# One half of the picks first, its expert rows summed during the other half's, and a third of the rows summed on the matrix engine

## The chip, the cores and the metric

The kernel runs on one core of a Trainium2 chip (trn2). The metric is the device time of one execution in microseconds (us). Five engines work beside each other: TensorE (PE; its weight loads are PEld in the profile), VectorE (DVE), ScalarE (ACT), GpSimd (POOL) and SyncE (SP). They meet only at semaphores. Transfers between device memory and the on-chip arena are made by 16 DMA engines; SP's queue issues those with fixed addresses, POOL's those that gather rows by an index.

## The reference, cut to what matters

A layer over T = 256 tokens of width D = 2048: a mixing half (RWKV scan, short convolution, projections), which the change does not touch, and then an expert half, in which each token picks 8 heads x 16 experts = 128 of 16384 experts:

```python
q = (h @ w_q)...; s1 = q[...,0,:] @ sub_keys_1; s2 = q[...,1,:] @ sub_keys_2
v1, i1 = top_k(s1, 16);  v2, i2 = top_k(s2, 16)          # per token and head
top, pos = top_k(v1[:, None] + v2[None, :], 16)           # of 256 sums
eidx = i1 * 128 + i2 (at pos);  gate = softmax(top)
act = gelu(einsum('td,tkd->tk', h, expert_u[eidx]))       # 128 dots per token
ff  = einsum('tk,tkd->td', gate * act, expert_v[eidx])    # 128 rows of 2048 summed per token
out = x + gate2 * rms_norm(ff, post_ffn_w)
```

Everything is float32. The 256 tokens are two blocks b of 128 tokens, one token on each partition. For each block and each k of 128, one gather brings one row per partition: 128 rows of `expert_v` are 1 MB, 256 gathers 256 MB.

## The kernel before

After the mixing half (about 800 us) the expert half runs in stages, and each engine's program is a fixed list with waits, so its order is the order of the source.

- Queries and routing. PE makes queries and scores in four groups g; ACT writes the scores (L752). DVE runs `route(b, g)` eight times (L1460 to L1507: MAX8, FIND_INDEX8, MATCH_REPLACE8 and small ops), each yielding 32 of the 256 indices (b, k).
- Dots. Of each `expert_u` row, 1152 columns are gathered by POOL (L544) into a ring of `UROWS` = 6 slots and multiplied with h by DVE (`dots`, L1527; 256 of them, numbered n). Between two routes stand 16 dots. The first `EARLY` = 48 take h from the arena (`junk`), the others from PSUM. The other 896 columns are done densely: SP loads 128 tiles (`product_tile`, 448 KB each, 4 slots), PE multiplies each with h of all 256 tokens (L1161) and ACT evacuates the result to `dense` (L761), 32768 columns of the arena.
- Picks. From `dense` the products of a token's own experts must be picked. In steps q of four tokens PE spreads the first keys (`spread_keys`, L1175, bfloat16), ACT turns them into one-hot rows (L775, L777), PE multiplies these with `dense` (L1189, float32, 4 matmuls) and DVE picks by the second key (`pick`, L1535). Two PSUM banks alternate in each of these. There are 64 steps; in every second one stands one of the last 32 dots (`LATE` = 224 - 128 = 96 of block 1).
- Sums. DVE adds both parts (L1558), ACT applies Gelu (L781), and DVE multiplies with the gates (L1563). Then for b in 0, 1 and k in 0..127: a gathered row of `expert_v`, times its weight, is added to sums in PSUM (L1573). POOL gathers into 12 slots of `v_row`, 8 of which lie in `dense`; its first gather waits for all 64 pick steps (`y_ps`), and each later one for the sum that frees its slot.
- End of a block: ACT takes squares and the root (L788 to L792), DVE scales and adds x (L1580, L1582), SP stores. x is parked in `out` and read back once `dense` is done with.

Of the kernel before, what the change touches and what calls it, by code (L numbers as in the profile page):

```python
# [99 lines left out]
def build_layer(nc, x, cols, ada, w_in, w_tail, lora_up, keys,  # L100
                u_dense, u_rows, expert_v, out):
    with ExitStack() as ctx:
# [100 lines left out]
        gw1 = new(D)  # L203
        junk = new(D)
# [3 lines left out]
        scores = [view(arena_size - (2 - b) * D, KC, NKEYS) for b in range(TB)]  # L208
# [6 lines left out]
        dense = view(dense_at, NKEYS, T)  # L215
        top[0] = ring_at
        tile_at = [take(KU * P), take(KU * P)]
        val1T = new(T)
        assert take(0) >= ring_at + SL
# [22 lines left out]
        gate, idx1f, idx2f = (view(front_at + n * TB * KTOP, TB, KTOP) for n in range(3))  # L242
        q_slot = [ring[:, 7, :], view(yT_at, D), view(yT_at + D, D), gw1]
        v_at = [g_at + (2 + n) * D for n in range(8)] + [row_at + n * D for n in range(4)]
        assert v_at[-1] + D <= dense_at and v_at[7] + D <= arena_size
        v_row = [view(a, D) for a in v_at]
        gw2, ff = view(dense_at, D), view(dense_at + D, D)
        assert dense_at + 2 * D <= g_at
# [60 lines left out]
        v_sum = sem("v_row_summed")  # L309
# [23 lines left out]
        def _(sp):  # L333
# [84 lines left out]
            sp.dma_start(xs[:, :, :], rows_of(out)).then_inc(x_in, 16)  # L418
            for tb in range(TB):
                for h in range(2):  # L420
                    c = slice(h * D // 2, (h + 1) * D // 2)
                    sp.wait_ge(fin_v, 4 * tb + 2 * (h + 1))
                    sp.dma_start(out[tb * P:(tb + 1) * P, c], xs[:, tb, c]).then_inc(stored, 16)
# [3 lines left out]
        def _(pool):  # L427
# [145 lines left out]
        def _(act):  # L573
# [168 lines left out]
            for g in range(4):  # L742
# [11 lines left out]
            for j in range(NKEYS):  # L754
                act.wait_ge(tile_ps, j + 1)
                if dense_at + (j + 1) * T > g_at and dense_at + j * T <= g_at:
                    act.wait_ge(stored, 16)
                    act.wait_ge(u_dot, EARLY)
                if dense_at + j * T == arena_size - 2 * D:
                    act.wait_ge(picked, 8)  # L760
                nc.scalar.activation(dense[:, j, :], bank(5 + j % 2, 0, T), ACT.Copy).then_inc(tile_out, 1)  # L761
# [8 lines left out]
            for q in range(T // 4):  # L770
# [8 lines left out]
            for b in range(TB):  # L779
                act.wait_ge(act_done, b + 1)  # L780
                nc.scalar.activation(wv[:, b, :], actv[:, b, :], ACT.Gelu).then_inc(gelu_done, 1)  # L781
            act.wait_ge(gw2_ps, 1)
            nc.scalar.activation(gw2, ps[:, 0:2048], ACT.Copy).then_inc(gw2_out, 1)
            for b in range(TB):
                act.wait_ge(v_sum, (b + 1) * KTOP)
                if b:
                    act.wait_ge(fin_v, 4 * b)
                nc.scalar.activation(ff, ps[:, 2048 - b * 2048:4096 - b * 2048], ACT.Square, accum_out=ss[:, 12 + b:13 + b]).then_inc(fin_a, 1)  # L788
# [3 lines left out]
                nc.scalar.activation(rstd[:, 12 + b:13 + b], lns[:, 12 + b:13 + b], ACT.Exp, scale=-0.5).then_inc(fin_a, 1)  # L792

        @block.tensor
        def _(pe):
# [297 lines left out]
            def rows(col, b0):  # L1093

                for k in range(KC):
                    last = mm(bank(b0 + k // 4, k % 4 * P, k % 4 * P + P), col[:, k:k + 1].broadcast_to([P, P]), ident, start=True, stop=True)
# [7 lines left out]
            p2.done(rows(gcol[:, 0, :], 2), "gate1")  # L1104
# [73 lines left out]
            pe.wait_ge(u_dot, KTOP)  # L1178
            spread_keys(0)
            for q in range(T // 4):  # L1180
                if q + 1 < T // 4:
                    spread_keys(q + 1)
# [5 lines left out]
                for i in range(4):  # L1188
                    last = mm(bank(5 + q % 2, i * P, (i + 1) * P), hot[q % 2][:, i, :], dense[:, :, 4 * q + i], start=True, stop=True)  # L1189
                last.then_inc(y_ps, 1)  # L1190

            pe.wait_ge(picked_out, T)
            pe.wait_ge(idxT_out, 1)
            for b in range(TB):
                last = nc.tensor.transpose(bank(7, b * P, (b + 1) * P), val1T[:, b * P:(b + 1) * P], ident)
            last.then_inc(valT_ps, 1)
            pe.wait_ge(u_dot, TB * KTOP)
            rows(gcol[:, 1, :], 0).then_inc(gw2_ps, 1)

        @block.vector  # L1200
        def _(dve):
# [256 lines left out]
            def top16(src, vals, where, rep):  # L1458
# [4 lines left out]
                r(V.match_replace(rep, vals[:, 0:8], src, NEG))  # L1463
                settle()
                r(V.max(vals[:, 8:16], rep))
                settle()
                r(V.max_index(where[:, 8:16], vals[:, 8:16], rep))  # L1467

            def route(b, g):

                dve.wait_ge(sc_out, 2 * g + b + 1)
                for c in range(4):
                    top16(scores[b][:, 4 * g + c, :], v16[:, c, :], u32(iu[:, c, :]), repl[:, c * NKEYS:(c + 1) * NKEYS])
# [7 lines left out]
                for h in range(2):  # L1481
                    top16(cand[:, h, :], topv[:, h, :], u32(pos[:, h, :]), repl[:, h * 256:(h + 1) * 256])
# [12 lines left out]
                for half, sel, dst in ((0, hi_f, idx1f), (1, lo_f, idx2f)):  # L1495
# [3 lines left out]
                    for h in range(2):  # L1499
                        e = eq[:, h * TOPK:(h + 1) * TOPK, :]  # L1500
                        r(tt(e, e, deep(i16[:, 2 * h + half, :]), ALU.mult))
                    settle()
# [17 lines left out]
            def dots(b, lo, hi):  # L1520

                for k in range(lo, hi):
                    n = b * KTOP + k
# [138 lines left out]
```

## Time and profile before

| | us |
|---|---|
| median of 3 runs (2208.21 to 2212.54) | 2210.57 |
| the profiled execution: its own time | 2209.84 |
| its span from first to last instruction | 2208.1 |
| DVE busy over the span | 1599.6 (72%) |
| PE busy | 1393.6 (63%) |
| POOL busy | 658.9 (30%) |
| ACT busy | 352.0 (16%) |
| DMA, mean over the span | 308 GB/s |

The profile's instants are us from the start of the span. Shares over the whole span mix stages with different limits, so the stages are read one by one: which engine is full, what rate the DMA moves, and what ended each wait. A float32 matmul is recorded as two instructions on PE. A DVE operation with an accumulator shows a short second record (DVE_READ_ACCUMULATOR); the distance of two starts is what one costs.

### The profile page before, as it was taken

Reading aid. Unit: us, or ns where it says so; the run is one execution under the profiler, and the core shown is the slowest. Engines: PE = TensorE matmul, PEld = TensorE weight load, DVE = VectorE, ACT = ScalarE, POOL = GpSimd, SP = SyncE. Lnnn points to the kernel's source line nnn. Section 1 sums busy time; section 2 is a strip of 40 time slices with the busy share of each in tenths; the row PEclk is TensorE's granted clock in tenths of the full one; section 3 lists DMA queues with packets and bytes.
Section 4 is the critical chain, followed back from the end, with each engine's and each line's share of the span. In section 5 each row is a group of like instructions: output and inputs, shape, how many; then the busy total and the mean of one; then the engine's idle time right before and its main releaser. Section 6 shows DMA issues by size and latency. Waiting matters only on the chain.

```text
span 2208.1 us, 20312 instructions
## 1 busy us (share of the span) xinstructions
PE 1393.6 (63%) x7103; PEld 1189.2 (54%) x7103; DVE 1599.6 (72%) x2429; ACT 352.0 (16%) x702; POOL 658.9 (30%) x707
## 2 busy tenths in 40 slices
PE   4799999999998989999999990499000000000000
PEld 4688888888885468888888880498000000000000
DVE  5945555655654023777778669988999998999998
ACT  2032222222221011011111120266000000000000
POOL 1022332213320001433322446422433333333331
PEclk8899999999999999999999995699555555555555
DMA  9936654565546553799998999854999999999995
GB/s 398 383 145 234 248 215 171 189 265 221 188 183 253 189 191 137 283 353 358 356 357 342 373 409 412 315 151 135 423 422 422 422 422 421 422 422 421 422 422 240
DMA packets 122001, 680.99 MB, mean 308 GB/s; under 512 B 13488, under 2 KB 13616, under 8 KB 65840
## 3 DMA queue, kind: packets, MB, share of 16 engines
q0 software_dynamic: 73728, 419.46, 47.1%
q1 hardware_dynamic: 47760, 257.97, 30.5%
q10 hardware_dynamic: 416, 2.25, 0.3%
q8 instruction: 62, 1.02, 0.2%
q14 instruction: 35, 0.29, 0.0%
HBM read 675.44 MB, written 4.19 MB: 308 GB/s over the span
## 4 chain that ended last, share of the span: by engine, by line
PE 38%; DMA 30%; DVE 27%; issue 2%; ACT 1%; POOL 1%; DVEq 0%; ACTq 0%; POOLq 0%
DVE ps L1573 15%; DMA arena<-in_u_rows,arena 15%; PE ps L868 14%; DMA arena<-in_expert_v,arena 13%; PE ps L1189 5%; PE ps L917 5%; PE ps L946 4%; DVE arena L1527 3%; DVE arena L1238 2%; PE ps L1087 2%; PE ps L951 2%; DMA arena<-in_ada 1%; PE ps L960 1%; DVE arena L1467 1%; DVE arena L1462 1%
## 5 line engine op out<-in xcount | busy, mean ns | idle before, releaser
L1573 DVE SCALAR_TENSOR_TENSOR ps<-arena,ps 128x2048 f32<-128x2048 f32 x256 | 602.8, 2355 | 36.3 <-DMA arena<-in_expert_v,arena 6.1
L1161 PE MATMUL ps<-arena 128*128 128x256 f32 x1792 | 387.1, 379 | 0.0
L544 POOL DMA_INDIRECT arena<-in_u_rows,arena x256 | 248.6, 971 | 444.7 <-DVE arena L1527 390.3
L1161 PEld LDWEIGHTS ps<-arena 128*128 128x128 f32 x1792 | 340.3, 190 | 46.5 <-DMA arena<-in_u_dense 0.3
L544 POOL DMA_INDIRECT arena<-in_expert_v,arena x256 | 239.9, 937 | 410.5 <-DVE ps L1573 380.0
L868 PE MATMUL ps<-arena 128*128 128x256 f32 x1440 | 339.3, 379 | 0.0
L1527 DVE SCALAR_TENSOR_TENSOR arena<-arena,ps 128x1152 f32<-128x1152 f32 x208 | 279.4, 1355 | 78.8 <-DMA arena<-in_u_rows,arena 74.4
L868 PEld LDWEIGHTS ps<-arena 128*128 128x128 f32 x1440 | 262.0, 190 | 29.4
L1189 PE MATMUL ps<-arena 128*128 128x128 f32 x512 | 124.9, 399 | 88.7 <-DVE ps L1535 86.3
L1189 PEld LDWEIGHTS ps<-arena 128*128 128x128 f32 x512 | 98.9, 207 | 93.3 <-DVE ps L1535 86.5
L1217 DVE SCALAR_TENSOR_TENSOR arena<-arena 128x2048 f32<-128x2048 f32 x60 | 142.8, 2381 | 0.0
L655 ACT ACTIVATE arena<-ps 128x512 f32<-128x512 f32 x144 | 81.7, 585 | 294.2 <-PE ps L951 116.3
L917 PE MATMUL ps<-arena 128*128 128x512 f32 x256 | 112.6, 593 | 1.5 <-DVE arena L1398 1.5
L1087 PE MATMUL ps<-arena 128*128 128x256 f32 x512 | 111.3, 379 | 0.0
L1358 DVE TENSOR_TENSOR arena<-ps,arena 128x512 f32<-128x512 f32 x40 | 27.7, 692 | 110.5 <-PE ps L946 110.5
L788 ACT ACTIVATE arena<-ps 128x2048 f32<-128x2048 f32 x2 | 3.8, 1877 | 642.9 <-DVE ps L1573 642.9
L1087 PEld LDWEIGHTS ps<-arena 128*128 128x128 f32 x512 | 96.9, 190 | 13.0
L761 ACT ACTIVATE arena<-ps 128x256 f32<-128x256 f32 x128 | 49.2, 384 | 339.5 <-PE ps L1161 339.5
L946 PE MATMUL ps<-arena 128*128 128x128 f32 x704 | 96.3, 280 | 4.3 <-ACT arena L655 3.1
L946 PEld LDWEIGHTS ps<-arena 128*128 128x128 f32 x704 | 89.0, 191 | 17.9 <-ACT arena L655 8.0
L1527 DVE SCALAR_TENSOR_TENSOR arena<-arena 128x1152 f32<-128x1152 f32 x48 | 64.4, 1360 | 45.1 <-DMA arena<-in_u_rows,arena 44.8
L517 POOL TENSOR_TENSOR arena<-arena 128x512 f32<-128x512 f32 x40 | 61.9, 1547 | 92.7 <-PE ps L946 92.7
(248 smaller groups left out, 1577.4 us busy)
## 6 DMA issues: line engine op xcount, KB each, us to landing
arena<-in_ada SPq DMA_DIRECT2D x96, 1024.0 KB, 5.0
arena<-in_u_dense SPq DMA_DIRECT2D x128, 448.0 KB, 6.9
arena<-in_w_in SPq DMA_DIRECT2D x45, 1024.0 KB, 6.7
arena<-in_w_tail SPq DMA_DIRECT2D x32, 1024.0 KB, 6.9
arena<-in_w_in SPq DMA_DIRECT2D x12, 512.0 KB, 16.7
arena<-in_u_rows,arena POOLq DMA_INDIRECT x256, 9.1
arena<-in_expert_v,arena POOLq DMA_INDIRECT x256, 25.4
arena<-in_x ACTq DMA_DIRECT2D x1, 2048.0 KB, 15.0
```

What stands on the lines that cost most here:

```text
L517: gm.done(tt(LTm[m % 2][:, :, :], LT[:, :, :], lmask[:, m:m + 1, :].broadcast_to([P, NCH, P]), ALU.mult), f"m{m}")
L544: nc.gpsimd.indirect_dma_start(out=row, out_offset=None, in_=table[:, :], in_offset=bass.IndirectOffsetOnAxis(ap=i32(idx[:, b, k:k + 1]), ...
L655: am.done(A(out, in_, func, **kw), name)
L868: last = mm(bank(b, 0, T), w[:, k, :], hT[:, k, :], start=(k == 0), stop=(k == KC - 1))
L917: last = mm(bank(OUT_BANKS[g][b]), yT[:, OUT_K[n], b * P:(b + 1) * P], w, start=(n == 0), stop=(n == KC - 1))
L946: last = mm(bank(b, c * P, c * P + P), l[:, c, :], r[:, c, :], start=True, stop=True)
L1087: last = mm(bank(b0 + s // 2, (s % 2) * T, (s % 2) * T + T), w[:, kk, s * P:(s + 1) * P], h2T[:, k, :], start=(k == 0 and s % 2 == 0), sto ...
L1161: last = mm(bank(5 + j % 2, 0, T), u_tile[j % len(u_tile)][:, k, :], h2T[:, k, :], start=(k == 0), stop=(k == KU - 1))
L1189: last = mm(bank(5 + q % 2, i * P, (i + 1) * P), hot[q % 2][:, i, :], dense[:, :, 4 * q + i], start=True, stop=True)
L1217: ins = stt(dst, ring[:, slot, :], silu_c[:, k:k + 1], dst, ALU.mult, ALU.add)
L1527: stt(row, row, 1.0, h, ALU.mult, ALU.mult, accum_out=actv[:, b, k:k + 1]).then_inc(u_dot, 1)
L1573: stt(sums_ps, v_row[n % len(v_row)], wv[:, b, k:k + 1], sums_ps, ALU.mult, ALU.add).then_inc(v_sum, 1)
```

## The change

Three things in the expert half. (1) `dense` is laid out as two halves, one per block, so the 32 pick steps of block 0 come first and free the first half; they carry 44 of the last 48 dots (`LATE` is now 256 - 48 = 208). Then block 0's activations and weights are made, and each pick step of block 1 is followed by three rows of block 0's sum. (2) Every third row (k % 3 == 2; 42 rows of block 0, 33 of block 1) is summed by PE: ACT scales the identity by the weights (`diagonal`), PE multiplies the row with it in four matmuls of 512 columns, accumulating in four PSUM banks, and DVE adds these banks to its own sum (`merge`), which now lies in the arena (`total`). (3) Dots stand inside `route`, two at 11 of 14 places, instead of 16 between routes. There are 13 row slots; three wait only for the last tile's product, four for the last dot, six for block 0's picks. Slots, scores, x and gate rows lie elsewhere, with waits to match.

```diff
+        dense = view(dense_at, TB, NKEYS, P)
+        diag = [view(front_at + 3 * TB * KTOP + T + n * P, P) for n in range(2)]
+        total = [view(half_at[0] + b * D, D) for b in range(TB)]
+        v_at = [0, D, ring_at] + [row_at + n * D for n in range(4)] + [half_at[0] + (TB + n) * D for n in range(6)]
+        V_EARLY, V_TILE = 7, 3
# POOL
                 if n == 0:
-                    pool.wait_ge(y_ps, T // 4)
-                if n == 8:
+                    pool.wait_ge(tile_ps, NKEYS)
+                if n == V_TILE:
                     pool.wait_ge(u_dot, TB * KTOP)
+                if n == V_EARLY:
+                    pool.wait_ge(y_ps, P // 4)
                 if n >= len(v_row):
-                    pool.wait_ge(v_sum, n - len(v_row) + 1)
+                    before = n - len(v_row)
+                    if on_pe(before):
+                        pool.wait_ge(d_sum, pe_rows(before) + 1)
+                    else:
+                        pool.wait_ge(v_sum, before - pe_rows(before) + 1)
# ACT
+                if g == 0:
+                    act.wait_ge(stored, 16)
...
-                if dense_at + (j + 1) * T > g_at and dense_at + j * T <= g_at:
-                    act.wait_ge(stored, 16)
+                if j == (junk_at - half_at[1]) // P:
                     act.wait_ge(u_dot, EARLY)
...
+            def diagonal(b, m):
+                d = b * PE_ROWS[0] + m
+                if d >= 2:
+                    act.wait_ge(d_sum, d - 1)
+                k = 3 * m + 2
+                nc.scalar.activation(diag[d % 2], ident, ACT.Copy, scale=wv[:, b, k:k + 1]).then_inc(diag_out, 1)
...
+            for q in range(P // 4 + 1):
+                one_hot(q)
+            gelu(0)
+            act.wait_ge(wv_done, 1)
+            for m in range(PE_ROWS[0]):
+                if P // 4 + 1 + m < T // 4:
+                    one_hot(P // 4 + 1 + m)
+                if m == P // 4 + 4:
+                    gelu(1)
+                diagonal(0, m)
+            act.wait_ge(wv_done, 2)
+            for m in range(PE_ROWS[1]):
+                if m == 4:
+                    norm(0, merged, 2)
+                    act.wait_ge(gw2_ps, 1)
...
+                diagonal(1, m)
+            norm(1, v_sum, TB * KTOP - sum(PE_ROWS))
# PE
+            def diagonal_row(b, m):
+                n = b * KTOP + 3 * m + 2
+                pe.wait_ge(diag_out, b * PE_ROWS[0] + m + 1)
+                pe.wait_ge(v_land[n % len(v_row)], 16 * (n // len(v_row) + 1))
+                for c in range(4):
+                    last = mm(bank(SUM_BANKS[b][c]), diag[(b * PE_ROWS[0] + m) % 2], v_row[n % len(v_row)][:, c * GROUP:(c + 1) * GROUP],
+                              start=(m == 0), stop=(m == PE_ROWS[b] - 1))
+                last.then_inc(d_sum, 1)
...
+            turn_products(0, 7)
+            for q in range(P // 4, T // 4):
+                if q + 1 < T // 4:
+                    spread_keys(q + 1)
+                key_rows(q)
+                if q == P // 4:
+                    pe.wait_ge(u_dot, TB * KTOP)
+                    pe.wait_ge(act_done, 1)
+                diagonal_row(0, q - P // 4)
# DVE
+            def some_dots():
+                calls[0] += 1
+                if calls[0] % 14 % 4 != 3:
+                    dots(ndot[0], ndot[0] + 2)
+                    ndot[0] += 2
             for c in range(1, 8):
-                dots(0, (c - 1) * 16, c * 16)
-                route(c // 4, c % 4)
+                route(c // 4, c % 4, some_dots)
+            dots(ndot[0], LATE)
...
+            for q in range(P // 4):
+                pick(q)
+                if q in (2, 4):
+                    gate_sums(q // 2 - 1)
+                more = 2 if q % 8 in (1, 4, 6) else 1
+                dots(ndot[0], ndot[0] + more)
+                ndot[0] += more
+            activations(0, 7)
+            dots(ndot[0], TB * KTOP)
+            weights(0)
+            for m in range(P // 4):
+                pick(P // 4 + m)
+                for k in range(3 * m, 3 * m + 3):
+                    add_row(0, k)
...
+            merge(0)
+            for k in range(KTOP):
+                if k == 12:
+                    finish(0)
+                if k == 3 * PE_ROWS[1] + 9:
+                    merge(1)
+                add_row(1, k)
+            finish(1)
+PE_ROWS = (KTOP // 3, 33)
+SUM_BANKS = ((2, 3, 4, 7), (0, 1, 5, 6))
```

`add_row` is the former sum (a plain multiply for k = 0) and passes over the rows that PE takes. The two MEMSETs of the PSUM sums are gone.

## Rows read from the trace of the kernel before

**Rows 1.** The page, second part: DMA rate in 40 slices of 55.2 us.
```profile
GB/s 398 383 145 234 248 215 171 189 265 221 188 183 253 189 191 137 283 353 358 356 357 342 373 409 412 315 151 135 423 422 422 422 422 421 422 422 421 422 422 240
```
**Rows 2.** Windows: from:to, length, busy of PE, PEld, DVE, ACT, POOL; clock, DMA, GB/s.
```profile
1200.00:1220.00 20.00, 20.00 (x95) 17.60 (x94) 19.04 (x71) 2.31 (x6) 1.90 (x3) 1.00 0.80 300
1240.00:1260.00 20.00, 20.00 (x95) 17.60 (x94) 11.25 (x19) 2.41 (x7) 8.45 (x9) 1.00 1.03 410
1440.00:1460.00 20.00, 20.00 (x121) 18.21 (x121) 17.73 (x91) 14.11 (x20) 4.70 (x5) 1.00 0.49 149
1900.00:2100.00 200.00, 0.00 (x0) 0.00 (x0) 191.19 (x82) 0.00 (x0) 76.39 (x82) 0.50 1.01 422
2180.00:2190.00 10.00, 0.00 (x0) 0.00 (x0) 9.58 (x5) 0.00 (x0) 0.00 (x0) 0.50 0.19 80
```
**Rows 3.** The page, fifth part: costliest groups.
```profile
L1573 DVE SCALAR_TENSOR_TENSOR ps<-arena,ps 128x2048 f32<-128x2048 f32 x256 | 602.8, 2355 | 36.3 <-DMA arena<-in_expert_v,arena 6.1
L1217 DVE SCALAR_TENSOR_TENSOR arena<-arena 128x2048 f32<-128x2048 f32 x60 | 142.8, 2381 | 0.0
L917 PE MATMUL ps<-arena 128*128 128x512 f32 x256 | 112.6, 593 | 1.5 <-DVE arena L1398 1.5
L1358 DVE TENSOR_TENSOR arena<-ps,arena 128x512 f32<-128x512 f32 x40 | 27.7, 692 | 110.5 <-PE ps L946 110.5
```
**Rows 4.** Timeline of all engines at both ends of the sums: start, length, what.
```profile
1536.38 0.94 POOL L544 DMA_INDIRECT arena<-in_expert_v,arena  x1 [20.54 <-PE ps L1189]
...
2194.95 1.88 ACT L788 ACTIVATE arena<-ps 128x2048 f32<-128x2048 f32 x1 [322.85 <-DVE ps L1573]
```
**Rows 5.** Timeline: ACT's first scores; then DVE's dots, one route, picks.
```profile
844.69 0.60 ACT L752 ACTIVATE arena<-ps 128x512 f32<-128x512 f32 x1 [6.67 <-PE ps L1135]
...
933.05 1.36 DVE L1527 SCALAR_TENSOR_TENSOR arena<-arena 128x1152 f32<-128x1152 f32 x1
...
1199.45 0.29 DVE L1460 MAX8 arena<-arena 128x8 f32<-128x128 f32 x1
...
1216.89 1.35 DVE L1527 SCALAR_TENSOR_TENSOR arena<-arena,ps 128x1152 f32<-128x1152 f32 x1
...
1218.16 1.35 DVE L1527 SCALAR_TENSOR_TENSOR arena<-arena,ps 128x1152 f32<-128x1152 f32 x1
...
1409.98 0.35 DVE L1535 SCALAR_TENSOR_TENSOR ps<-arena,ps 128x128 f32<-128x128 f32 x1
...
1410.25 0.35 DVE L1535 SCALAR_TENSOR_TENSOR ps<-arena,ps 128x128 f32<-128x128 f32 x1
```
**Rows 6.** Source views: tiles, x's store, row gathers (ns min/median/max, first and last start).
```profile
L1161 PE MATMUL ps<-arena x1792: 379/379/483, 930.1 to 1316.9; 128*128 128x256 f32 x200
...
L406 SPq DMA_DIRECT2D out<-arena x1: 399/399/399, 800.5 to 800.5; - x1
...
DMA to landing us min/median/max: 14.2/14.2/14.2
...
L544 POOL DMA_INDIRECT arena<-in_expert_v,arena x256: 932/939/948, 1536.4 to 2165.3; - x128
```
**Rows 7.** Timelines of DVE and of POOL: dots from the arena, gathers beside them.
```profile
985.14 1.36 DVE L1527 SCALAR_TENSOR_TENSOR arena<-arena 128x1152 f32<-128x1152 f32 x1 [0.38 <-DMA arena<-in_u_rows,arena]
...
986.69 1.36 DVE L1527 SCALAR_TENSOR_TENSOR arena<-arena 128x1152 f32<-128x1152 f32 x1 [0.19 <-DMA arena<-in_u_rows,arena]
...
985.87 1.44 POOL L544 DMA_INDIRECT arena<-in_u_rows,arena  x1 [0.30 <-issue]
987.61 1.25 POOL L544 DMA_INDIRECT arena<-in_u_rows,arena  x1 [0.30 <-issue]
```
**Rows 8.** Windows, columns as in Rows 2: PE in a pause, at half clock, at full.
```profile
800.00:802.00 2.00, 0.00 (x0) 0.00 (x0) 1.83 (x4) 1.94 (x5) 0.00 (x0) 0.50 0.98 410
...
804.00:806.00 2.00, 2.00 (x11) 2.00 (x10) 0.67 (x1) 0.00 (x0) 0.00 (x0) 0.50 1.10 369
...
808.00:810.00 2.00, 2.00 (x12) 1.79 (x11) 2.00 (x5) 2.00 (x5) 0.00 (x0) 1.00 0.98 410
```

More of the change, by code:

```diff
@@ L203, in build_layer @@
         gw1 = new(D)
+        junk_at = take(0)
         junk = new(D)
@@ L207, in build_layer @@
         qT = view(q_at, KC, T)
-        scores = [view(arena_size - (2 - b) * D, KC, NKEYS) for b in range(TB)]
+        scores = [view(arena_size - (1 - b) * NKEYS * P - D, KC, NKEYS) for b in range(TB)]
         i32 = lambda v: v.bitcast(I32)
@@ L1091, in groups, with rows @@
                         score(g - 1)
-            def rows(col, b0):
+            def rows(col, banks):
                 for k in range(KC):
-                    last = mm(bank(b0 + k // 4, k % 4 * P, k % 4 * P + P), col[:, k:k + 1].broadcast_to([P, P]), ident, start=True, stop=True)
+                    last = mm(bank(banks[k // 4], k % 4 * P, k % 4 * P + P), col[:, k:k + 1].broadcast_to([P, P]), ident, start=True, stop=True)
                 return last
@@ L1103, in _ @@
             pe.wait_ge(v2.sem, v2.at("ga1"))
-            p2.done(rows(gcol[:, 0, :], 2), "gate1")
+            p2.done(rows(gcol[:, 0, :], (2, 3, 4, 5)), "gate1")
             for g in range(1, 4):
@@ L1188, in _ @@
                 for i in range(4):
-                    last = mm(bank(5 + q % 2, i * P, (i + 1) * P), hot[q % 2][:, i, :], dense[:, :, 4 * q + i], start=True, stop=True)
+                    b, t = divmod(4 * q + i, P)
+                    last = mm(bank(5 + q % 2, i * P, (i + 1) * P), hot[q % 2][:, i, :], dense[:, b, :, t], start=True, stop=True)
                 last.then_inc(y_ps, 1)
-            pe.wait_ge(picked_out, T)
-            pe.wait_ge(idxT_out, 1)
-            for b in range(TB):
-                last = nc.tensor.transpose(bank(7, b * P, (b + 1) * P), val1T[:, b * P:(b + 1) * P], ident)
@@ L1200, in _ @@
+            turn_products(1, 0)
+            for m in range(P // 4, PE_ROWS[0]):
+                diagonal_row(0, m)
+            pe.wait_ge(act_done, 2)
+            for m in range(PE_ROWS[1]):
+                diagonal_row(1, m)
+                if m == 1:
+                    pe.wait_ge(merged, 2)
+                    rows(gcol[:, 1, :], SUM_BANKS[0]).then_inc(gw2_ps, 1)
         @block.vector
@@ L1456, in _, with top16 @@
             NEG = -3.0e38
-            def top16(src, vals, where, rep):
+            def top16(src, vals, where, rep, between):
                 r(V.max(vals[:, 0:8], src))
@@ L1501, in route @@
                         r(tt(e, e, deep(i16[:, 2 * h + half, :]), ALU.mult))
+                    between()
                     settle()
@@ L1518, in gate_sums, with dots @@
                 settle()
-            def dots(b, lo, hi):
-                for k in range(lo, hi):
-                    n = b * KTOP + k
+            def dots(lo, hi):
+                for n in range(lo, hi):
+                    b, k = divmod(n, KTOP)
+                    if n == EARLY:
+                        dve.wait_ge(h_ps, 1)
                     row = u_row[n % UROWS]
@@ new lines, in merge, with finish @@
+            def merge(b):
+                dve.wait_ge(d_sum, sum(PE_ROWS[:b + 1]))
+                dve.wait_ge(v_sum, nsum[0])
+                at = 0
+                for lo, hi in ((2, 5), (7, 8)) if b == 0 else ((0, 2), (5, 7)):
+                    c = slice(at, at + (hi - lo) * GROUP)
+                    tt(total[b][:, c], ps[:, lo * GROUP:hi * GROUP], total[b][:, c], ALU.add).then_inc(merged, 1)
+                    at = c.stop
+                dve.wait_ge(merged, 2 * (b + 1))
+            def finish(b):
@@ L1598, with on_pe, pe_rows @@
 EARLY = 48
-LATE = KTOP - T // 8
+LATE = TB * KTOP - 48
+PE_ROWS = (KTOP // 3, 33)
+SUM_BANKS = ((2, 3, 4, 7), (0, 1, 5, 6))
+def on_pe(n):
+    b, k = divmod(n, KTOP)
+    return k % 3 == 2 and k < 3 * PE_ROWS[b]
+def pe_rows(n):
+    return sum(on_pe(i) for i in range(n))
 def kernel(x, c, ada_w, ada_b, pre_mix_w, post_mix_w, w_in, rwkv_mix, w0, w_up, a0, a_up, g_up, k_k, k_a, r_k,
```

123 lines of the change are left out of this document (63 added, 60 removed).

## Prediction

> **What bounds the kernel now.** I began with the DMA rate in slices [rows 1]: from slice 29 on, a third of the span, it stands at 422 GB/s, and it falls to 151 and 135 in the two slices just before. So I asked stage by stage which engine was full and whether the DMA was [rows 2]. Four stages matter:
> - Routing and dots, to about 1217. PE is busy all the time (the tiles), while DMA moves 300 GB/s beside a route and 410 beside dots: the ring of 6 fills while DVE routes, and then nothing asks.
> - Dots alone, 1217 to 1410: DMA at 412 in the slice from 1325 [rows 1], DVE waits for rows. DMA-bound.
> - Picks, 1410 to 1537: PE full, DVE 89%, DMA at 149 GB/s. PE-bound; DMA half idle.
> - Sums: DMA at 422 and DVE at 96% [rows 2]. One row is 1.049 MB, so DMA needs 2.485 us a row, and DVE 2.355 [rows 3] plus about 0.10 between two, 2.46. Both are bounds within 1%, so quicker sums alone can gain only DVE's lag: the last row has landed at about 2182 (0.19 of the window that begins at 2180 [rows 2]), DVE ends at 2195 [rows 4].
>
> What a gain must come from is therefore DMA time that is idle before the sums, from 1410 to 1537 and beside the routes.
>
> **Part 1, routing between dots.** A route is 17.4 us (1199.45 to 1216.89), a dot 1.28 (start to start) [rows 5]. Now a route carries 22 dots: 17.4 + 22 x 1.28 = 45.6 us of DVE, 2.07 us a dot. DMA beside the tiles: a tile takes (1316.9 - 930.1) / 128 = 3.02 us [rows 6] for 0.459 MB, 152 GB/s; of 410 [rows 2] 258 are left, and a row of 0.590 MB takes 2.29 us. So DMA, not DVE, sets the pace, if the ring never runs dry. At 933 the kernel before starts dot 21 [rows 5]; with dots in the route by then done (DVE allows up to 28) I take 25. Then (1317 - 933) / 2.29 = 168 more by the last tile, 193; the 15 left to dot 208 at 0.590 MB / 412 GB/s = 1.43 us end at 1338. Before, dot 224 ended at 1409.98 [rows 5], dot 208 thus at 1410 - 16 x 1.43 = 1387. Bounds: 1336 and 1387 (no gain, if dots in program order wait for rows while routing queues behind them). I take 1348, near the first, since DVE has 10% slack but the ring covers only 6 rows. Two waits are added or moved here. ACT's wait for x's store stands before the scores, and routing and PE's next scores wait behind it; the store lands at 815 and the scores come at 844.7 [rows 5, 6]: 30 us of cover, nothing. The wait for dot 48 stands before tile 29, at 933 + 29 x 3.02 = 1020, dot 48 comes at 933 + 23 x 2.29 = 986: 34 us of cover; past it, PE's tiles would stop and all behind them.
>
> **Part 2, block 0's picks.** A pick is 0.27 [rows 5]. DVE: 128 x 0.27 + 44 x 1.28 + the two gate sums (three small operations each, estimated at 1.1 from the route's small ones) = 34.6 + 56.3 + 2.2 = 93 us. PE takes 1.98 us a step (91 DVE records in 20 us at 18 for two steps [rows 2]), 63 us: covered. So DVE sets it, and DMA again has slack (44 rows in 93 us). Row gathers begin once the gather of dot 256 is out, which waits for dot 250: 1348 + 90 = 1438, where they began at 1536.4 [rows 4]. Three rows fit before the last dots end; those come after block 0's activations, some 7 us behind the picks, and row 4 may be late by 3 us.
>
> **Part 3, the sums.** Before, first gather to last landing took 2182 - 1536.4 = 645.6 us, 636 of rows and the rest x read back and a store. These stay. With DMA the bound, the last row lands at 1438 + 645.6 + 3 = 2087. Each three rows give 7.455 us; what must fit in:
> - DVE, with block 1's picks: 4 x 0.27 + 2 x 2.48 (arena form, 2.381 [rows 3], plus 0.10) = 6.0. It fits.
> - PE: a 512-column matmul is two instructions of 112.6 / 256 = 0.44 [rows 3], 8 of them 3.5 us, and a pick step 1.98: 5.5. It fits at full clock.
> - ACT: two passes over the one-hot rows and a diagonal, under 2 us. Free.
> - POOL: a gather is 0.94 [rows 6] and 0.30 of issue [rows 7]: 3 x 1.24 = 3.7. It fits.
> - Slots: 13 x 2.485 = 32 us round; a row is held up to 7 us by DVE or PE, which leaves ten in flight. `finish(0)`, the gate rows (PE) and `norm(0)` (ACT, with later diagonals queued behind it, and PE's rows behind those) hold some for perhaps 15 us; before, the same steps stood between two sums, and no slice there leaves 422 [rows 1].
>
> At the end PE has left; DVE takes 29 rows alone at 2.48 against 2.485, with `merge(1)` in the way: 4 x 0.69 [rows 3] = 2.8. So the last sum ends 2.4 + 2.8 = 5.2 after the last landing, where it was 13. From there to the end 2208.1 - 2194.95 = 13.2 [rows 4], unchanged.
>
> **Sum.** 2087 + 5.2 + 13.2 = 2105.4 of span, 103 under 2208.1: about 39 from the routes, 59 from the picks (net of dots moved into them), 8 from DVE's lag, less 3. The profiled execution's own time is 1.7 above its span, and it is 0.7 under the median: 2107 us.
>
> **Gathers beside sums from the arena.** In the kernel before, a gather that is issued while DVE runs a dot with both inputs in the arena is stretched: 1.44 and 1.25 us, each ending 0.81 after the dot did [rows 7]. Beside the present sums, with one input in PSUM, the longest of 256 took 0.948 [rows 6]. The new sums have both in the arena, so a gather waits for up to one sum. It gets through at the dot's end, with 0.19 us before the next one [rows 7]; so one passes per sum, and 2 per three rows plus two in the 2.5 us that DVE has left. That is 4 for 3 needed, and I cost it at nothing.
>
> The Trainium skill, "SBUF — State Buffer", section "Who interferes with whom", says that a DVE instruction with two SBUF inputs and a GpSimd instruction that reads SBUF shut each other out for a whole instruction. The stretched gathers agree, with their 0.81 us after the dot; that DVE is shut out in turn, no row here shows. By the rule alone the gathers would be late, which is rival B.
>
> **Rivals.**
> A. TensorE at half clock in block 1's picks. For: after a pause the clock was 0.50, and stayed so in a window in which PE was busy throughout, before it rose [rows 8]; in the new stage PE has gaps of 2 us each 7.5. Against: PE has some 75% to do there. At 1.2 GHz the row costs 7.0 and the step at least 1.98 (0.2 by the weight loads): 9.0 to 9.4 against 7.455, 32 times: 50 to 62 us, 2163. Behind the picks 7.0 still fits. The skill ("TensorE: Matmul & The Clock Gate", section "What's actually happening") has PE start at half clock after an idle spell and reach full after sustained work; by it each wait for a row could count, which is this case.
> B. The slower side: gathers get through only while DVE rests. Place: the gap of 0.10 us between two sums, half of the one seen. Price: three gathers need 3 x 1.24 of rest, so three rows take 4.96 + 3.72 = 8.7, 1.2 more than 7.455, 75 times, plus 16 rows at the end at 1.2: 110 us. 2217, slower by 0.3%. It decides when three rows cost more than about 8.6. Partial forms (gathers late, some bubbles) give 2120 to 2170.
> C. Dots in the routes bring nothing, because DVE waits in program order: 1387 for 1348, 2146.
> D. PE cannot hide its weight loads (8 x (0.85 + 0.2) at half clock, 8.4; with picks 10.6): 32 x 3.1 + 43 x 0.95 = 140 us, 2247.
>
> **How the numbers follow.** Forecast (DMA sets the pace, 2088 to 2130): 0.56; C and mixtures to 2150: 0.14; A: 0.12; B partial: 0.08; B full: 0.05; D: 0.05. Likeliest 2107. Low end 2088: dot 208 at 1336, no gap, merge hidden. High end 2170, past A; beyond are B in full and D. A measurement can tell 0.2%, some 4 us, from no change: faster 0.88, same 0.03, slower 0.09.
>
> **What would show it.** Right: DMA at 410 beside the routes without the dips to 300; the first pick near 1348; the first row gather near 1438; 422 GB/s from there to about 2087; POOL waiting for DVE and PE; clock 1.00 in block 1's picks. Wrong: DMA under 400 after the first rows. Then the waits tell: DVE for PE with clock 0.50 is A or D; gathers of 2 to 3 us with DVE waiting for landings is B; a first pick near 1387 is C.

## The result and the profile after

The changed kernel takes 2102.46 us (median of 4 runs, 2101.11 to 2104.54), the kernel before in the same comparison 2209.73 (2208.21 to 2212.54): a ratio of 0.951, 95% interval 0.950 to 0.953, or 107 us less. The forecast was 2107. The profiled execution, the slowest of the four, took 2104.54 us, its span 2102.7. The kernel before was timed again with each group of runs below (medians 2209.88, 2210.53 and 2211.90); each ratio is to the one of its own group, and differences of about 2 us between groups are not read.

The page of the changed kernel: DMA rate and granted clock in 40 slices of 52.6 us, and three groups of instructions (busy us, mean ns | idle before).

```profile
PEclk8899999999999999999999999677999988888865
...
GB/s 395 407 143 270 223 148 203 262 216 168 211 265 195 227 153 160 203 322 410 409 409 407 409 407 409 344 296 368 421 422 421 421 422 421 423 422 421 422 422 277
...
L1657 DVE SCALAR_TENSOR_TENSOR arena<-arena 128x2048 f32<-128x2048 f32 x179 | 420.8, 2351 | 125.8 <-DMA arena<-in_expert_v,arena 113.8
L550 POOL DMA_INDIRECT arena<-in_expert_v,arena x256 | 406.6, 1588 | 220.7 <-PE ps L1244 115.3
L1244 PE MATMUL ps<-arena 128*128 128x512 f32 x600 | 348.6, 735 | 168.0 <-DMA arena<-in_expert_v,arena 165.3
```

Against [rows 1]: beside the tiles and routes the 410 is now held where it was 342 to 373, and the trough before the sums, once 315, 151 and 135, is 344, 296 and 368. From there the rate is 422 as before, so the sums did not get quicker; they started 103 us sooner (first row gather at 1433.8, before at 1536.4). DVE now makes 179 sums instead of 256 [rows 3], beside two plain multiplies, and waits 114 us for rows, which is time that it has over. A gather's mean is 1588 ns where the longest was 948 [rows 6]. It is stretched, and it costs nothing that the rate would show.

Windows of the changed kernel (columns as in Rows 2): beside a route, beside tiles, in block 0's picks, at the first sums, in block 1's picks, in block 1's sums.

```profile
1200.00:1220.00 20.00, 20.00 (x94) 17.60 (x94) 15.15 (x38) 2.30 (x6) 7.84 (x9) 1.00 1.03 409
1240.00:1260.00 20.00, 20.00 (x94) 17.62 (x93) 11.81 (x19) 2.68 (x7) 9.10 (x10) 1.00 1.03 411
1380.00:1400.00 20.00, 16.00 (x84) 14.10 (x84) 20.00 (x77) 9.87 (x14) 9.17 (x10) 0.76 0.89 290
1440.00:1460.00 20.00, 13.20 (x37) 7.04 (x38) 10.80 (x23) 3.40 (x6) 14.86 (x13) 0.69 1.00 416
1500.00:1600.00 100.00, 84.70 (x265) 46.13 (x264) 75.76 (x132) 22.14 (x39) 71.12 (x39) 0.90 1.01 421
1900.00:1950.00 50.00, 32.55 (x54) 12.98 (x55) 30.88 (x14) 2.41 (x6) 26.16 (x19) 0.81 1.01 422
```

The first line stands against 300 GB/s in [rows 2], the fifth against 149 in the picks. In block 1's picks DVE is busy 76% and PE 85%, and DMA is the only one that is full. In block 0's picks DVE is full (20.00 of 20.00) and DMA has slack, as the prediction had it.

Timeline of the changed kernel: the first pick, row gathers, the first sum by scalar-tensor-tensor, the first rows on PE, the end of the last sums. They answer to [rows 4, 5].

```profile
1343.57 0.35 DVE L1613 SCALAR_TENSOR_TENSOR ps<-arena,ps 128x128 f32<-128x128 f32 x1
...
1433.80 0.94 POOL L550 DMA_INDIRECT arena<-in_expert_v,arena  x1 [0.30 <-issue]
1435.05 0.94 POOL L550 DMA_INDIRECT arena<-in_expert_v,arena  x1 [0.30 <-issue]
1436.29 0.94 POOL L550 DMA_INDIRECT arena<-in_expert_v,arena  x1 [0.31 <-issue]
1441.49 0.93 POOL L550 DMA_INDIRECT arena<-in_expert_v,arena  x1 [4.26 <-DVE arena L1605]
...
1444.17 2.35 DVE L1657 SCALAR_TENSOR_TENSOR arena<-arena 128x2048 f32<-128x2048 f32 x1 [0.35 <-DMA arena<-in_expert_v,arena]
1446.76 6.42 PE L1244 MATMUL ps<-arena 128*128 128x512 f32 x8 [9.20 <-DMA arena<-in_expert_v,arena]
1455.23 3.71 PE L1244 MATMUL ps<-arena 128*128 128x512 f32 x8
...
2038.12 2.35 DVE L1667 TENSOR_TENSOR arena<-ps,arena 128x1024 f32<-128x1024 f32 x2
2040.51 49.00 DVE L1657 SCALAR_TENSOR_TENSOR arena<-arena 128x2048 f32<-128x2048 f32 x20
...
2089.54 1.91 ACT L811 ACTIVATE arena<-arena 128x2048 f32<-128x2048 f32 x1 [85.28 <-DVE arena L1657]
```

The third gather started at 1436.3, the fourth waited 4.26 us for the last dot (L1605). The last line is ACT's first pass behind the last sum; the end is 13.2 us later, as in [rows 4].

### The profile page after: what moved, and what is told of

It reads as the page before. It is cut to its first block, busy times and chain, and to the rows that moved or that the text cites. A ratio compares the mean times of both kernels' runs of the same rounds, so it can differ in the third digit from the quotient of the medians.

```text
span 2102.7 us, 21519 instructions
## 1 busy us (share of the span) xinstructions
PE 1749.5 (83%) x7703; PEld 1326.7 (63%) x7703; DVE 1404.0 (67%) x2356; ACT 377.9 (18%) x778; POOL 834.3 (40%) x707
## 4 chain that ended last, share of the span: by engine, by line
PE 37%; DMA 36%; DVE 18%; POOL 5%; issue 3%; ACT 1%; DVEq 0%; ACTq 0%; POOLq 0%
DMA arena<-in_expert_v,arena 19%; DMA arena<-in_u_rows,arena 15%; PE ps L911 14%; DVE arena L1605 7%; PE ps L960 5%; POOL arena L550 5%; PE ps L989 4%; PE ps L1244 3%; DVE arena L1657 3%; DVE arena L1311 2%; DVE ps L1613 2%; PE ps L1130 2%; PE ps L994 2%; DMA arena<-in_ada 1%; PE ps L1003 1%
## 5 line engine op out<-in xcount | busy, mean ns | idle before, releaser
L1657 DVE SCALAR_TENSOR_TENSOR arena<-arena 128x2048 f32<-128x2048 f32 x179 | 420.8, 2351 | 125.8 <-DMA arena<-in_expert_v,arena 113.8
L550 POOL DMA_INDIRECT arena<-in_expert_v,arena x256 | 406.6, 1588 | 220.7 <-PE ps L1244 115.3
L1244 PE MATMUL ps<-arena 128*128 128x512 f32 x600 | 348.6, 735 | 168.0 <-DMA arena<-in_expert_v,arena 165.3
L550 POOL DMA_INDIRECT arena<-in_u_rows,arena x256 | 257.6, 1006 | 350.4 <-DVE arena L1605 291.2
L1204 PEld LDWEIGHTS ps<-arena 128*128 128x128 f32 x1792 | 340.4, 190 | 46.2
L1244 PEld LDWEIGHTS ps<-arena 128*128 128x128 f32 x600 | 134.7, 236 | 366.9 <-issue 341.9
L1605 DVE SCALAR_TENSOR_TENSOR arena<-arena,ps 128x1152 f32<-128x1152 f32 x208 | 278.2, 1350 | 62.6 <-DMA arena<-in_u_rows,arena 60.0
L911 PEld LDWEIGHTS ps<-arena 128*128 128x128 f32 x1440 | 262.0, 190 | 29.4
L1290 DVE SCALAR_TENSOR_TENSOR arena<-arena 128x2048 f32<-128x2048 f32 x60 | 142.8, 2380 | 0.0
L1230 PEld LDWEIGHTS ps<-arena 128*128 128x128 f32 x512 | 103.1, 235 | 44.6 <-DVE ps L1613 37.0
L960 PE MATMUL ps<-arena 128*128 128x512 f32 x256 | 114.0, 599 | 1.5 <-DVE arena L1471 1.5
L1613 DVE SCALAR_TENSOR_TENSOR ps<-arena,ps 128x128 f32<-128x128 f32 x256 | 74.0, 349 | 55.0 <-PE ps L1230 46.1
L1130 PEld LDWEIGHTS ps<-arena 128*128 128x128 f32 x512 | 96.9, 190 | 13.0
L989 PEld LDWEIGHTS ps<-arena 128*128 128x128 f32 x704 | 89.0, 191 | 17.9 <-ACT arena L667 8.0
```

The costliest lines, as they stand in the source:

```text
L550: nc.gpsimd.indirect_dma_start(out=row, out_offset=None, in_=table[:, :], in_offset=bass.IndirectOffsetOnAxis(ap=i32(idx[:, b, k:k + 1]), ...
L911: last = mm(bank(b, 0, T), w[:, k, :], hT[:, k, :], start=(k == 0), stop=(k == KC - 1))
L960: last = mm(bank(OUT_BANKS[g][b]), yT[:, OUT_K[n], b * P:(b + 1) * P], w, start=(n == 0), stop=(n == KC - 1))
L989: last = mm(bank(b, c * P, c * P + P), l[:, c, :], r[:, c, :], start=True, stop=True)
L1130: last = mm(bank(b0 + s // 2, (s % 2) * T, (s % 2) * T + T), w[:, kk, s * P:(s + 1) * P], h2T[:, k, :], start=(k == 0 and s % 2 == 0), sto ...
L1204: last = mm(bank(5 + j % 2, 0, T), u_tile[j % len(u_tile)][:, k, :], h2T[:, k, :], start=(k == 0), stop=(k == KU - 1))
```

## Experiments

Each run undoes or does one part, or puts a price on one suspected cost. The three runs behind the first heading measure the parts, the next one puts rival B to the test, and the others look for what the stream of rows can bear. In the diffs "..." stands for lines left out.

### Where the 107 us come from

**Routing alone, from both sides.** First the changed kernel with the dots back between the routes:

```diff
-                route(c // 4, c % 4, some_dots)
+                dots(ndot[0], ndot[0] + 16)
+                ndot[0] += 16
+                route(c // 4, c % 4)
```

> The changed kernel with its dots between the routes again, 16 at a time, as in the kernel before; order of picks and TensorE's share of the sums stay. My theory (DMA sets the pace, and each part pays by starting the stream of expert_v rows earlier): the first pick, at 1344 in the changed kernel, comes at 1387 again, the first row gather 43 us later than 1434, the rest of the span as it was, so about 2146 us. Rival (the time came from the order of the picks and from TensorE, and DMA between the routes would have caught up anyway): under 2115 us.

Measured 2150.15 us (2149.27 to 2151.3), ratio to before 0.973 (0.971 to 0.975): 47.7 more than the changed kernel. The first pick came at 1388.5 instead of 1343.6, and the first row gather at 1478.8 instead of 1433.8, 45 later both, where 43 was expected.

Then the kernel before, with its routes given the same hook and nothing else:

```diff
             for c in range(1, 8):
-                dots(0, (c - 1) * 16, c * 16)
-                route(c // 4, c % 4)
+                route(c // 4, c % 4, some_dots)
...
```

> The kernel before with one part of the change alone: two dots at 11 of 14 places in each route. My theory: dot 224 at about 1367 in place of 1410, everything behind it 43 us earlier, about 2167 us; the saving is the same with the old order of picks, because it is DMA time that was idle beside the routes. Rival (the saving needs the new order behind it): within 15 us of the kernel before.

Measured 2165.10 us (2163.79 to 2166.55), ratio 0.980 (0.978 to 0.981): 44.8 less than before. The DMA rate on the two pages, first the changed kernel without dots in routes, then the kernel before with them:

```profile
GB/s 396 389 166 242 231 171 197 240 230 194 175 235 216 235 180 75 339 273 356 341 328 350 365 410 411 406 280 333 422 422 421 421 422 422 422 422 421 422 422 285
```
```profile
GB/s 396 385 163 239 234 193 171 236 247 212 162 206 214 252 211 42 359 351 410 409 409 408 404 410 395 242 145 208 422 422 421 422 422 421 423 422 422 422 422 236
```

The 328 to 365 beside routes comes back in the one and goes in the other. The trough of 145 stays in the second, since its 64 pick steps still stand in one stage that PE bounds (PE busy 120.00 us of the 120 from 1370 to 1490, 133 GB/s). Rival C (dots in routes bring nothing) is out, and the part acts by itself: 45 to 48 us in either kernel.

**TensorE's share taken away.** In the changed kernel DVE sums every row; diagonals, PE's rows and both merges are gone, and the making of the gate rows and block 0's norm move to the places that this leaves.

```diff
-PE_ROWS = (KTOP // 3, 33)
+PE_ROWS = (0, 0)
-                diagonal_row(0, q - P // 4)
...
-            merge(0)
```

> The changed kernel with all 256 rows summed on VectorE; no diagonals, no matmuls for rows, no merges. My theory (two near-equal bounds, DMA 2.485 and VectorE 2.46 us a row): VectorE now sets the end. From the first sum at 1444: 32 steps of picks at 1.07, 256 sums at 2.455, 5 us for the end of block 0 and some 2 us of small steps give 2113, and 13.2 us behind it 2126 of span, about 2128 us: TensorE's share of the sums is worth only some 25 us of the 107. Rival (TensorE's taking 75 rows of 2.46 us off VectorE, 184 us, is what pays): 2180 us or more.

Measured 2121.8 us (2119.2 to 2122.2), ratio 0.960 (0.958 to 0.961). So PE's rows, with what moved beside them, are worth 19.3 us where I expected some 25, and the new order of picks and rows without them 43.3 (from 2165.1). Windows of this kernel in block 1's picks and behind them, and its gathers:

```profile
1500.00:1600.00 100.00, 30.23 (x144) 25.89 (x144) 96.80 (x133) 17.27 (x25) 89.03 (x37) 0.50 0.99 378
1700.00:1900.00 200.00, 5.96 (x32) 5.77 (x32) 189.81 (x86) 7.32 (x9) 174.72 (x84) 0.52 1.01 422
```
```profile
L550 POOL DMA_INDIRECT arena<-in_expert_v,arena x256 | 570.1, 2227 | 81.9 <-issue 77.7
```

Where picks stand between sums, DVE is at 97% and the rows come at 378 GB/s; that is the shortfall PE's share removes. From 1440 to 1700 it comes to some 23 us of the DMA's time, and from the first row gather to the last landing this kernel took about 671 us, some 22 more than the changed one. Behind the picks DVE alone holds 422, though nearly each gather is stretched.

The three steps 44.8 + 43.3 + 19.3 = 107.4 add up by construction, since they are differences of neighbouring medians; that the route's part is the same from both sides is the only check on them. The middle step holds everything that is neither dots in routes nor PE's rows, the slots and the places in the arena too, and what PE's rows would bring without the new order was not tried.

### Gathers beside sums from the arena

The kernel before, with only the place of the sums changed from PSUM to the arena, so that each sum now has both inputs in the arena (and the end of a block reads the sums there):

```diff
+        total = [view(dense_at + (2 + b) * D, D) for b in range(TB)]
...
-                sums_ps = ps[:, 2048 - b * 2048:4096 - b * 2048]
+                sums_ps = total[b]
```

> The kernel before with one thing changed: the sums of the expert_v rows lie in the arena and not in PSUM, so each sum on VectorE has both inputs in the arena, and VectorE has only 0.10 us between two of them. My theory: a waiting gather gets through in that gap, one per sum, 2.45 us each with its issue; DMA still sets the pace and the time is the same, 2206 to 2216 us, while the mean gather grows from 0.94 to some 2.1 us. Rival B of the prediction (a gather gets through only while VectorE rests): a row costs 2.46 + 1.24 = 3.7 us, about 300 us more, 2500 us.

Measured 2210.79 us (2207.63 to 2212.81, 10 runs), ratio 1.0005 (0.9994 to 1.0015): no difference. Its groups and a window in the sums:

```profile
L1574 DVE SCALAR_TENSOR_TENSOR arena<-arena 128x2048 f32<-128x2048 f32 x256 | 602.0, 2351 | 36.5 <-DMA arena<-in_expert_v,arena 5.9
L545 POOL DMA_INDIRECT arena<-in_expert_v,arena x256 | 540.2, 2110 | 111.7 <-issue 78.0
```
```profile
1900.00:2100.00 200.00, 0.00 (x0) 0.00 (x0) 191.10 (x82) 0.00 (x0) 174.74 (x82) 0.50 1.01 422
```

A gather goes from 937 ns on the page of before to 2110 and fills POOL, yet 82 gathers meet 82 sums in 200 us, one for one, at 422 GB/s. A sum took 2351 ns where it took 2355 [rows 3]: DVE is not shut out in turn. The gathers of this kernel end 0.81 us after a sum does (one at 1952.37, the sum at 1951.56), into the next sum. So one gather passes for each gap of 0.10 us between two sums, which is what rival B denied.

### What the stream of rows needs

**Eight slots instead of thirteen.**

```diff
-... + [half_at[0] + (TB + n) * D for n in range(6)]
+... + [half_at[0] + (TB + n) * D for n in range(1)]
```

> The changed kernel with 8 slots for expert_v rows in place of 13. My theory: what a slot must cover is the time that a row is held (7 us by VectorE or TensorE), the stretched gather (up to 3 us) and a landing; 8 x 2.485 = 20 us covers that inside a block, and falls short only where block 0 ends and in the first rows, so 2103 to 2120 us. Rival (the slots were the tight place, and the larger ring carries part of the gain): every row waits, DMA under 400 GB/s throughout, 2150 us or more.

Measured 2104.93 us (2102.67 to 2106.59), ratio 0.952 (0.951 to 0.954), against 0.951 with 13 slots: the medians are 2.5 us apart, and the ranges overlap. A window over 1460 to 1700 shows 421 GB/s. Down to eight slots, the depth of the ring is not what holds the rate here.

**PE's rows twice.** Each of TensorE's rows is multiplied a second time. It then counts twice in the sum, so the result is wrong and only the time is of use:

```diff
-                for c in range(4):
+                for i in range(8):
+                    c = i % 4
...
-                              start=(m == 0), stop=(m == PE_ROWS[b] - 1))
+                              start=(m == 0 and i < 4), stop=(m == PE_ROWS[b] - 1 and i >= 4))
```

> The changed kernel with each of TensorE's rows multiplied twice (8 matmuls in place of 4; its rows then count twice in the sum). It gives TensorE the 7.0 us a row that rival A had at half clock. My theory: beside block 1's picks three rows take 7.0 + 1.98 = 9.0 us in place of 7.455, 32 times, 50 us more, and behind the picks 7.0 still fits under 7.455: about 2152 us. Rival (TensorE and VectorE overlap so well that nothing is lost, or the handshakes add up): 2110 us or less, or 2200 us or more.

Measured 2139.99 us (2138.83 to 2141.36), ratio 0.968 (0.967 to 0.970), 37.5 over the changed kernel. The profiled spans differ by 34.4, but this execution made its first row gather 3.6 us sooner (1430.25); from there to the end it took 38 more. Windows in block 1's picks (four) and in block 1's sums:

```profile
1500.00:1520.00 20.00, 19.88 (x61) 10.21 (x60) 12.74 (x29) 3.80 (x8) 10.16 (x7) 1.00 1.01 422
1540.00:1560.00 20.00, 19.93 (x62) 10.18 (x61) 13.07 (x22) 3.40 (x6) 10.48 (x7) 1.00 0.90 351
1500.00:1600.00 100.00, 99.58 (x305) 51.30 (x304) 63.54 (x110) 17.71 (x33) 52.83 (x33) 1.00 0.93 365
1600.00:1700.00 100.00, 99.55 (x303) 51.56 (x302) 63.55 (x110) 18.41 (x33) 52.51 (x33) 1.00 0.91 345
1800.00:1900.00 100.00, 95.03 (x241) 42.05 (x240) 67.67 (x33) 12.00 (x21) 53.42 (x43) 1.00 1.01 422
```

PE is full and sets the pace: its doubled rows follow each other at 9.19 us (1472.89, 1482.07, 1491.25), where 9.0 was expected. But 32 steps at 9.19 instead of 7.455 should have cost 55 us, and cost 38; the time came out 12 under the expected 2152. The windows show where the rest went. PE takes 9.19 a step from the start of the stage, yet DMA holds 422 GB/s until 1520: it runs ahead of PE. Only then it falls to 351 and below, and from 1520 to 1740 POOL waits 89 us for sums of DVE that free a slot. DMA's shortfall against 422 adds up to 39 us from 1440 to 1740. Behind the picks PE stays full at 20.00 of 20 us until 1800 beside 422 GB/s, so it works off rows that lie ready. The difference of 17 us is some seven rows of lead. That the lead is as long as it is because of the 13 slots was not tried with another number. This stretch is what rival A would have made, so A was priced too high, at 50 to 62 for about 38.

### What is left at the start of the rows

**Three rows early.** Three slots wait for nothing but the last tile's product, and DMA has slack in block 0's picks. So their gathers are issued behind the dots' gathers 228, 232 and 236:

```diff
-            for n in range(TB * KTOP):
+                if n == 228:
+                    pool.wait_ge(tile_ps, NKEYS)
+                if n in (228, 228 + 4, 228 + 8):
+                    early = (n - 228) // 4
+                    gather(v_row[early], expert_v, 0, early, v_land[early])
+            for n in range(V_TILE, TB * KTOP):
...
```

> The changed kernel with the gathers of the first three expert_v rows issued among the last dots' gathers (behind those of dots 228, 232, 236), since their slots are free from the last tile on and DMA moves only 290 GB/s during block 0's picks. My theory (DMA sets the pace from the first row on): the stream ends three rows earlier, 3 x 2.485 = 7.5 us, about 2095 us. Rival (the stream's start is set by VectorE's first sum at 1444, which stays, or the dots' rows come late): 2100 to 2105 us, no change.

Measured 2101.83 us (2100.07 to 2103.20), ratio 0.951 (0.949 to 0.952): nothing gained, and my expectation of 2095 fell. A window and the fourth gather:

```profile
1430.00:1440.00 10.00, 2.70 (x13) 2.37 (x13) 9.96 (x31) 1.56 (x3) 1.71 (x3) 0.50 0.32 110
```
```profile
1438.74 0.94 POOL L550 DMA_INDIRECT arena<-in_expert_v,arena  x1 [7.99 <-DVE arena L1608]
```

The rows do come early, but the fourth slot waits for the last dot, as before, and DMA rests meanwhile: 110 GB/s where the changed kernel has 301, and 0 from 1434 to 1440. The three rows' time has only moved.

**The slots' order as well.** On top of the last edit, the six slots in block 0's half of `dense`, free once its picks are made, now come before the four that wait for the last dot:

```diff
-        v_at = [0, D, ring_at] + [row_at + n * D for n in range(4)] + [half_at[0] + (TB + n) * D for n in range(6)]
+        v_at = [0, D, ring_at] + [half_at[0] + (TB + n) * D for n in range(6)] + [row_at + n * D for n in range(4)]
...
                 if n == V_TILE:
+                    pool.wait_ge(y_ps, P // 4)
+                if n == V_HALF:
                     pool.wait_ge(u_dot, TB * KTOP)
-                if n == V_EARLY:
-                    pool.wait_ge(y_ps, P // 4)
```

> The three early rows of the run before this one, and the row slots in another order: behind the three that are free from the last tile on come the six in block 0's half of the dense products (free once its pick steps are multiplied, near 1430), then the four that wait for the last dot (near 1439). In the run with early rows alone DMA fell to 110 GB/s from 1430 to 1440: the fourth row waited for the last dot. My theory (that gap took back what the early rows gave, and DMA sets the pace else): 422 GB/s from about 1432 without a gap, the last row lands some 12 to 15 us before that of the changed kernel, 2087 to 2092 us. Rival (VectorE's start of the sums at 1441 and its pace in the last 29 rows set the end, not DMA): 2098 to 2103 us, the same as without.

Measured 2096.28 us (2092.76 to 2098.61, 5 runs), ratio 0.948 (0.946 to 0.949): 6.2 us faster than the changed kernel, with no overlap of the ranges. It is a gain, but under the expectation of 2087 to 2092, and just outside the rival's 2098 to 2103. Its windows in block 0's picks and at their end, and its next gathers:

```profile
1390.00:1400.00 10.00, 8.43 (x47) 7.16 (x46) 10.00 (x43) 4.72 (x7) 5.64 (x6) 0.84 1.00 409
1430.00:1440.00 10.00, 2.90 (x14) 2.37 (x13) 10.00 (x26) 0.31 (x1) 6.76 (x8) 0.53 0.91 299
```
```profile
1433.22 0.94 POOL L550 DMA_INDIRECT arena<-in_expert_v,arena  x1 [0.30 <-issue]
1434.46 0.94 POOL L550 DMA_INDIRECT arena<-in_expert_v,arena  x1 [0.30 <-issue]
```

Now the wait is gone, and its stream ends at about 2074.5 instead of 2082.6. Of these 8 us, 0.9 is that this execution began its dots sooner (865.9 against 866.8), which leaves 7.2; three rows at 2.485 are 7.5. I had expected 12 to 15, with 422 GB/s from 1432 on. The row above shows 299 from 1430 to 1440, no more than the 301 of the changed kernel; why the rate stays there until 1440, with gathers going out each 1.24 us, was not found.

**The order alone**, with the same lines of slots and waits and nothing early:

> The changed kernel with the other order of slots alone, no early rows: after three rows at 1434 to 1437 the six in block 0's half go out at once, where the changed kernel waits until 1441.5 for the last dot. My theory: DMA's gap there is 2 to 4 us, so 2098 to 2101 us. Rival (VectorE sets the end): no change, 2102 to 2103 us.

Measured 2101.90 us (2100.20 to 2103.99), ratio 0.950 (0.949 to 0.952): nothing, where I had expected 2098 to 2101. It was timed in one group with the run before, which is 5.6 us faster with ranges that do not meet; that pair shows the early rows' worth most cleanly. VectorE's program is the same in both, so it does not set the end, as the rivals of these runs had it. In the changed kernel the three gathers of 1433.8 to 1436.3 bring 7.5 us of work, behind what the dots still have under way, and the fourth comes at 1441.5, about when that is done; there is hardly a gap to close. Only both edits together gain: the early rows make the gap, and the order fills it.

## Why the prediction was right, and where it was off

**The steps.** The time of the profiled execution can be put together as the prediction did:

| step | forecast | measured |
|---|---|---|
| dot 208 done, first pick | 1348 | 1343.6 |
| from there to the first row gather | 90 | 90.2 |
| block 0's picks | 93 | 92.3 |
| first row gather | 1438 | 1433.8 |
| from there to the last landing | 649 | 648.8 |
| last landing to the end of the last sum | 5.2 | 6.9 |
| to the end of the span | 13.2 | 13.2 |
| span | 2105.4 | 2102.7 |

The last landing is read from two windows of the changed kernel:

```profile
2080.00:2082.00 2.00, 0.00 (x0) 0.00 (x0) 2.00 (x1) 0.00 (x0) 0.00 (x0) 0.50 0.78 324
2082.00:2084.00 2.00, 0.00 (x0) 0.00 (x0) 1.90 (x2) 0.00 (x0) 0.00 (x0) 0.50 0.32 131
```

The second moved 0.62 us' worth of 422 GB/s, so 2082.6; since the first had already fallen to 324, this is good to about half a microsecond. Between the two profiled spans the first row gather came 102.6 us sooner, the stream took 3.2 longer and the lag fell by 6.0: 105.4 together.

**Part 1.** The mechanism held and its gain was sized too low: 39 forecast, 45 measured between the two kernels that differ only in it (the changed one and the one with dots between routes). What the order and PE's rows bring together was 64 in the forecast (59 and 8, less 3) and is 62.6 measured (2165.10 - 2102.46). So the sum is near in part because the two misses, 6 too low and 1.4 too high, have opposite signs. I had added 10 us to the near bound for a ring of six that might run dry. It did not; DMA held 409 in a route. The near bound of 1338 (the sum's own; the list of bounds has 1336) with the 2.9 us by which this execution started its dots later (866.8 against 863.9) makes 1341; measured 1343.6. Dot 48 was done at 988.8 (986 forecast), well before tile 29.

**Part 2.** Right in size and in the engine that sets it. What I had called a possible delay of row 4 is there as 4.26 us of POOL waiting, but it cost nothing, since three rows were on their way. The 3 us that the sum adds for it came true by luck: the stream did take 648.8 us instead of 645.6, but in the kernel with the order alone, where POOL does not wait for the last dot, it takes 648.6 too (1432.35 to about 2081). The record does not settle what these 3 us are. One difference is on it: the last dot's row gather goes out 1.2 us before the first `expert_v` gather (1432.6), where in the kernel before it went out 21 us ahead (1514.9), so now rows of dots are still under way. 3.2 us at 422 GB/s are 1.35 MB, or 2.3 of their rows; that this is the cause fits, but no run shows it. The same wait made a miss in the run with three rows early, where I had not asked what the fourth slot waits for.

**Part 3.** The stream came out within 1 us, with that luck in it. DVE's lag was 1.7 longer: `merge(1)` took 2.4 (2038.12 to 2040.51), 0.4 less than forecast, but before it DVE stood some 5 us behind the landings and not 2.4. This comes from 6.9, plus the 0.7 that 20 sums at 2.45 gain on landings at 2.485, less the 2.4. Why a further 2.5 us lay there was not tried. The lag fell by 6 us and not by 8.

**Rival A** came true in part. The clock was 0.90 in block 1's picks, not 1.00. PE's rows there, then windows of 2 us and the rows behind them later in the changed kernel:

```profile
1552.80 3.68 PE L1244 MATMUL ps<-arena 128*128 128x512 f32 x8 [1.76 <-DMA arena<-in_expert_v,arena]
1560.27 5.37 PE L1244 MATMUL ps<-arena 128*128 128x512 f32 x8 [1.78 <-DMA arena<-in_expert_v,arena]
1567.72 3.67 PE L1244 MATMUL ps<-arena 128*128 128x512 f32 x8
```
```profile
1900.00:1902.00 2.00, 0.44 (x1) 0.47 (x2) 1.33 (x1) 0.00 (x0) 0.40 (x1) 0.50 1.03 430
1908.00:1910.00 2.00, 0.98 (x3) 0.54 (x4) 0.77 (x1) 0.01 (x1) 1.70 (x2) 1.00 1.01 418
```
```profile
1901.56 6.00 PE L1244 MATMUL ps<-arena 128*128 128x512 f32 x8 [4.73 <-DMA arena<-in_expert_v,arena]
1909.02 3.67 PE L1244 MATMUL ps<-arena 128*128 128x512 f32 x8 [1.45 <-DMA arena<-in_expert_v,arena]
```

After a wait of 4.73 us a row ran most of its length at half clock (0.50, that is 1.2 GHz; 0.93 in its last window, 1906 to 1908) and took 6.00; after one of 1.45 it ran at full clock (2.4 GHz) and took 3.67. The wait just before does not settle it alone: in block 1's picks a row took 3.68 after 1.76 us and the next one 5.37 after 1.78. The Trainium skill, "TensorE: Matmul & The Clock Gate", section "What's actually happening", has PE start slow after an idle spell; this trace agrees, with 0.50 after the wait of 4.73 us. Yet 5.37 and a pick step of 1.98 are 7.35, still under the 7.455 of three landings: these rows start 7.47 and 7.45 apart, slow or not, and the rate stays at 421. So the half clock cost nothing. As the doubled rows show, that cover is gone when every step in block 1's picks takes 9.19.

**Rival B** falls with the sums moved in the kernel before, **C** with the routing from both sides. For **D**, PE's group of rows has a mean of 735 ns, 8 x 0.735 = 5.9 at the mean clock with the half-clock rows in it, and PE waits 165 us for landings. D had 8.4 at half clock; the longest of the rows shown, the first, took 6.42. The Trainium skill, "SBUF — State Buffer", section "Who interferes with whom", has the two engines shut each other out for a whole instruction. The runs bear out one side, gathers of 2.15 us, and not the other: each sum begins while a gather is still 0.81 us from its end, and yet DVE takes 2351 ns and the ratio is 1.0005.

## What to carry to other kernels

When a transfer-bound stage is near its limit, look for time in which the DMA engines rest before it, and cost the change by when that stage can start; here the first gather of the sums came 102.6 us sooner, of 105.4 between the two profiled spans. Before an extra transfer is put early, ask what the next one waits for: time gained for three rows is lost again if the fourth stands at the same wait, and a reordering that gains nothing alone can be the other half of one that does. Here an engine that grew slower cost nothing while its share lay within the transfer's time; to price such a suspicion, double the suspected share and see what it costs.

## What had not been expected of the hardware

- A row gather beside a sum with both inputs in the arena takes 2.15 us instead of 0.94, and still one passes per sum through a gap of 0.10 us. In the changed kernel's last gathers, one starts each 2.45 us, as the sums do, at 422 GB/s:

```profile
2046.43 2.15 POOL L550 DMA_INDIRECT arena<-in_expert_v,arena  x1 [0.30 <-issue]
2048.88 2.15 POOL L550 DMA_INDIRECT arena<-in_expert_v,arena  x1 [0.30 <-issue]
2051.34 2.15 POOL L550 DMA_INDIRECT arena<-in_expert_v,arena  x1 [0.30 <-issue]
```

- Under a load that comes and goes with a period of 7.5 us, TensorE's clock did not settle: the mean is 0.81 over 1900 to 1950, and the windows of 2 us from 1900 to 1914 have 0.50 three times, 0.93 once and 1.00 three times.
